# Two transformer blocks on one Trainium2 core: norm vectors moved into modulation columns, residual and gate moved into the experts' accumulators

## The chip, the cores and the metric

One core of one Trainium2 chip. The metric is the device time of one execution in microseconds (us), over which all weights are streamed once from HBM. Three runs of the kernel before gave a median of 1635.99 us (1635.38 to 1636.00). The engines are called TensorE (PE in the profile), VectorE (DVE), ScalarE (ACT), GpSimd (POOL) and SyncE (SP, which issues the loads); PEld are TensorE's weight loads.

## The reference

256 tokens of width 1024, all in float32. Block one is a parallel mixer, a cross attention and a mixture of experts, each added to x, then an RMS norm:

```
h = rms(x)*g_mix;  q,k,v,su,sv,ga,gb = split(h @ w_in)        # 3840 columns
q,k = rope(rms(q)*g_q), rope(rms(k)*g_k)
merged = sigmoid(ga)*(gqa(q,k,v) @ w_att_out) + sigmoid(gb)*(sgu(gelu(su),gelu(sv)) @ w_sgu_out)
x += merged @ w_out
x += cross(rms(x)*g_cross @ w_cq, rms(mem)*g_mem @ w_ckv) @ w_co
x += moe(rms(x)*g_moe)          # 16 experts, 2 per token, width 512
x = rms(x)*g_final
```

Block two has four sublayers s = 0..3: stick-breaking attention (16 heads), MoE, retention (8 heads, group norm, silu gate), MoE. The shift, scale and gate of each come from `silu(c) @ ada_w[s] + ada_b[s]`, 3 x 1024 numbers per sublayer:

```
x = layer_norm(alpha*x + gate_s * f_s(x*(1+scale_s) + shift_s)) * ln_g[s] + ln_b[s]     # alpha = 4**0.25
stick breaking: softplus(z) = max(z,0) + ln(1 + exp(-|z|)), its suffix sums are exponents of the weights
```

## The kernel before

**Data.** `X` (128 partitions x 2 token tiles x 1024) holds the residual stream, `XN` an RMS-normalised copy in block one. Weights arrive as 2 MB panels. A dense fp32 product is built from fp32r parts: ScalarE rounds a panel by quarters into `WHI` (`split_next`, L1117), GpSimd subtracts to `WLO` (`split_low`, L2030), and TensorE adds three products per piece. Activations are turned by `transposes` (L388, 128x128 through the identity) and split into `HTH` (ScalarE) and `HTL` (VectorE) by `turn_split` (L1132, L1486). In block two the turn also applies scale and shift, which stand as columns in `ADA` (channel on the partition).

**Loads.** SyncE issues everything in the order of `stream` (L233 ff.). Non-expert panels go round three slots of `ring_lo`: a load waits until the split of the panel three before it has read its slot. Experts use six slots. 24 panels belong to the modulation (`ada_w`, six per sublayer: two each for shift, scale and gate); `ADA_AFTER` says behind which panel each stands. TensorE takes one by `ada_panel` (L505): 8 fp32 products with silu(c) as the weights, then ScalarE copies the sums to `AROW` (`ada_copy`), TensorE turns them to columns, VectorE adds the bias (`ada_sum`, L1542). `keep_warm(n)` (L522) issues n idle products of 512 columns. SyncE also issues small vectors behind named panels (`small`); VectorE waits for all 13 of these ahead of the norm of q and k. `LNG` holds one pair of row vectors, broadcast over partitions, for the next norm's gain and bias (`gains`, L1031).

**MoE.** `moe(L)` runs on each engine: transposes of `XN` (L = 0) or `X`, router product, VectorE's choice of two experts per token, slots by a rank product, `XSPLIT` (high rows by ScalarE, low rows by GpSimd, `rows_low`, L2045), then 16 experts in 8 pairs with an extra block for overfull experts. Per expert: gather, gate and up, silu, turn, down into bank `B_Y`, `yh_out` (ScalarE) and `yl_out` (VectorE) scale by the token's weight and split, and a scatter product adds into four PSUM accumulators of 512 columns, which zero products open. After MoE 0 `residual` (L1657) adds them to X; after MoE 1 and 2 `deepnorm` (L1872) multiplies by the gate rows in `GB` (made by a diagonal and `gate_rows`, L659), adds alpha*X, takes moments, normalises, and applies gain and bias.

**Stick-breaking.** For 16 heads TensorE gives z; ScalarE takes |z|, Exp by groups of four, then four Ln of 1536 columns (three table loads with the Exp that follows); then a loop over heads: `weights` (VectorE), a suffix-sum product, Exp, value product; `values_out` copies head h-5.

**Retention.** Per head: scores, decay (VectorE), values, `stats`, `gated` (subtract mean, times silu(g)) and an in-place scaling by rstd, all on VectorE; when all 8 are done TensorE turns 16 chunks and `ret_out` runs.

The code that sets the extent of the zero products before, and the wait of q's norm:

```
for i in list(range(4)) * (2 if L else 4):
    ins = mm(acc[i], YH[0][:, 0:P], YH[0], True, False)
...
dve.wait_ge(S("small_in"), 16 * 13)
```

## Time and profile before

| what | us |
|---|---|
| median of 3 runs | 1635.99 |
| profiled execution | 1636.46 |
| its span | 1634.70 |
| TensorE busy | 1481.1 (91%) |
| VectorE busy | 532.0 (33%) |
| ScalarE busy | 463.4 (28%) |
| GpSimd busy | 423.6 (26%) |
| mean HBM traffic over the span | 273 GB/s |

The profiled execution's own time holds 1.76 us more than its span. Engines' busy times overlap, so their shares don't add up; a stage is read from a window that holds it alone. Matmul records overlap as well, and a row of the timeline can stand for several instructions (x4) of one line that follow one another.

### The profile page before, as it was taken

Reading aid. Unit: us, or ns where it says so; the run is one execution under the profiler, and the core shown is the slowest. Engines: PE = TensorE matmul, PEld = TensorE weight load, DVE = VectorE, ACT = ScalarE, POOL = GpSimd, SP = SyncE. Lnnn points to the kernel's source line nnn. Section 1 sums busy time; section 2 is a strip of 40 time slices with the busy share of each in tenths; the row PEclk is TensorE's granted clock in tenths of the full one; section 3 lists DMA queues with packets and bytes.
Section 4 is the critical chain, followed back from the end, with each engine's and each line's share of the span. In section 5 each row is a group of like instructions: output and inputs, shape, how many; then the busy total and the mean of one; then the engine's idle time right before and its main releaser. Section 6 shows DMA issues by size and latency. Waiting matters only on the chain.

```text
span 1634.7 us, 21298 instructions
## 1 busy us (share of the span) xinstructions
PE 1481.1 (91%) x7787; PEld 916.9 (56%) x7788; DVE 532.0 (33%) x1077; ACT 463.4 (28%) x792; POOL 423.6 (26%) x190
## 2 busy tenths in 40 slices
PE   7889988999999989879879999989994999999974
PEld 5777666744444479656434444369883864444431
DVE  5395424411111220236312222337008072222114
ACT  3544334211112133632211112145441321111110
POOL 5783443200000067032000000059953710000000
PEclk9999989899999989999989999989998979999997
DMA  7644365689999955518449999965541276999940
GB/s 260 226 170 154 130 238 199 254 362 426 428 429 429 374 204 199 213 37 335 169 172 423 430 428 428 365 247 194 202 158 52 103 326 260 423 429 428 429 197 26
DMA packets 89976, 447.77 MB, mean 274 GB/s; under 512 B 8212, under 2 KB 10152, under 8 KB 71336
## 3 DMA queue, kind: packets, MB, share of 16 engines
q1 hardware_dynamic: 88320, 446.17, 68.7%
q8 instruction: 55, 0.90, 0.2%
q10 hardware_dynamic: 1576, 0.49, 0.1%
q14 instruction: 25, 0.20, 0.0%
HBM read 445.60 MB, written 1.05 MB: 273 GB/s over the span
## 4 chain that ended last, share of the span: by engine, by line
PE 62%; issue 20%; DVE 11%; ACT 3%; POOL 3%; DMA 1%; DVEq 0%; POOLq 0%; ACTq 0%
PE ps L386 58%; POOL WLO L2042 2%; DVE ST L1448 1%; PE ps L718 1%; PE ps L758 1%; ACT WHI L1130 1%; PE ps L739 1%; DVE X L1889 1%; DVE X L1890 1%; DVE Z L1992 1%; PE ps L396 1%; DVE X L1883 1%; DVE SM L1880 1%; DVE Z L1580 1%; DVE Z L1581 1%
## 5 line engine op out<-in xcount | busy, mean ns | idle before, releaser
L2042 POOL TENSOR_TENSOR WLO<-ring_lo,WHI 128x1024 fp32r<-128x1024 f32 (+1 forms) x160 | 389.9, 2458 | 252.6 <-ACT WHI L1130 252.6
L386 PE MATMUL ps<-ring_hi,Z 128*64 128x512 f32 x1248 | 283.7, 604 | 5.4 <-DVE Z L1810 3.0
L386 PE MATMUL ps<-ring_lo,Z 128*64 128x512 f32 x1152 | 260.0, 601 | 5.3 <-issue 5.3
L2028 POOL TENSOR_TENSOR RS<-MS,NEGH 128x2 f32<-128x2 f32 (+1 forms) x19 | 16.1, 848 | 916.8 <-DVE MS L1458 635.9
L1130 ACT ACTIVATE WHI<-ring_lo 128x1024 fp32r<-128x1024 f32 (+1 forms) x160 | 164.6, 1048 | 234.4 <-PE ps L386 220.1
L386 PE MATMUL ps<-WHI,HTH 128*128 128x512 f32 (+1 forms) x448 | 178.4, 398 | 17.8 <-POOL WLO L2042 14.8
L386 PEld LDWEIGHTS ps<-ring_hi,Z 128*64 128x64 f32 x1248 | 88.7, 139 | 176.4 <-issue 169.8
L386 PE MATMUL ps<-WLO,HTH 128*128 128x512 f32 (+1 forms) x448 | 176.5, 394 | 0.0
L386 PE MATMUL ps<-WHI,HTL 128*128 128x512 f32 (+1 forms) x448 | 175.9, 393 | 0.0
L386 PEld LDWEIGHTS ps<-ring_lo,Z 128*64 128x64 f32 x1152 | 82.2, 138 | 156.0 <-issue 155.7
L1813 DVE TENSOR_TENSOR Z<-ps,Z 64x512 f32<-64x512 f32 x50 | 34.7, 694 | 327.1 <-ACT Z L1281 327.1
L1281 ACT ACTIVATE Z<-ps 64x512 f32<-64x512 f32 x50 | 29.5, 590 | 340.9 <-PE ps L386 340.9
L386 PEld LDWEIGHTS ps<-WHI,HTH 128*128 128x128 f32 x448 | 86.5, 193 | 38.7 <-issue 19.1
L386 PEld LDWEIGHTS ps<-WHI,HTL 128*128 128x128 f32 x448 | 86.5, 193 | 17.9
L386 PEld LDWEIGHTS ps<-WLO,HTH 128*128 128x128 f32 x448 | 86.7, 194 | 17.1
L386 PE MATMUL ps<-HTH,WHI 128*128 128x256 f32 x320 | 93.0, 291 | 0.6 <-DVE ADA L1550 0.6
L1816 DVE SCALAR_TENSOR_TENSOR YLS<-ps,Z,YHS 128x512 fp32r<-128x512 f32 x50 | 37.6, 751 | 169.0 <-ACT YHS L1287 169.0
L386 PE MATMUL ps<-HTH,WLO 128*128 128x256 f32 x320 | 91.3, 285 | 0.0
L386 PE MATMUL ps<-HTL,WHI 128*128 128x256 f32 x320 | 91.2, 285 | 0.0
L1287 ACT ACTIVATE YHS<-ps,Z 128x512 fp32r<-128x512 f32 x50 | 34.4, 687 | 184.2 <-PE ps L386 184.2
L1149 ACT ACTIVATE Z<-ps 128x512 f32<-128x512 f32 (+1 forms) x88 | 45.5, 553 | 75.6 <-PE ps L386 65.2
L386 PEld LDWEIGHTS ps<-HTH,WHI 128*128 128x128 f32 x320 | 62.5, 195 | 1.9 <-issue 1.3
(258 smaller groups left out, 1821.9 us busy)
## 6 DMA issues: line engine op xcount, KB each, us to landing
ring_lo<-in_ada_w SPq DMA_DIRECT2D x24, 2048.0 KB, 8.1
ring_lo<-in_moe_w_gate SPq DMA_DIRECT2D x16, 2048.0 KB, 10.6
ring_lo<-in_moe_w_up SPq DMA_DIRECT2D x16, 2048.0 KB, 15.0
ring_lo<-in_moe_w_down SPq DMA_DIRECT2D x16, 2048.0 KB, 14.1
ring_hi<-in_moe_w_gate SPq DMA_DIRECT2D x16, 2048.0 KB, 11.9
ring_hi<-in_moe_w_up SPq DMA_DIRECT2D x16, 2048.0 KB, 16.3
ring_hi<-in_moe_w_down SPq DMA_DIRECT2D x16, 2048.0 KB, 13.7
ring_lo<-in_ret_w_in SPq DMA_DIRECT2D x12, 2048.0 KB, 8.1
```

Of the source, the lines that this page charges most:

```text
L386: return nc.tensor.matmul(o, l, r, start=start, stop=stop, skip_group_check=True)
L396: ins = nc.tensor.transpose(o[:, at:at + P], src(t, c), ident)
L718: ins = nc.tensor.transpose(ps[:, bank, j * P:(j + 1) * P], ROWS[h][:, j * P:(j + 1) * P], ident)
L739: ins = nc.tensor.transpose(ps[:, bank, t * P:(t + 1) * P], sel[:, t, :], ident)
L758: ins = nc.tensor.transpose(ps[:, B_GU, c * CAP:(c + 1) * CAP], by4[CAP:P, c, :], CST[CAP:P, C_ID + CAP:C_ID + P])
L1130: nc.scalar.activation(WHI[:, q, 0:size], slot(r)[:, q * size:(q + 1) * size], Copy).then_inc(S("hi_split"), 1)
L1149: drain(nc.scalar.activation(dst, o[:, src], func, **k), key)
L1281: nc.scalar.activation(SG[a][CAP:P, :], ps[0:CAP, B_GU, :], ACT.Silu).then_inc(done, 1)
L1287: nc.scalar.activation(YH[a], ps[:, B_Y, :], Copy, scale=WSLOT[a]).then_inc(done, 1)
L1813: V.tensor_tensor(HH[a][CAP:P, :], ps[CAP:P, B_GU, :], SG[a][CAP:P, :], ALU.mult).then_inc(done, 1)
L1816: V.scalar_tensor_tensor(out=YL[a], in0=ps[:, B_Y, :], scalar=WSLOT[a], in1=YH[a].bitcast(F32), op0=ALU.mult, op1=ALU.subtract).then_inc(d ...
L2042: nc.gpsimd.tensor_tensor(WLO[:, q, 0:size], slot(r)[:, q * size:(q + 1) * size], WHI[:, q, 0:size].bitcast(F32), ALU.subtract).then_inc(S ...
```

## The change

- `ADA_AFTER` and the calls that use up the panels: new places for 20 of the 24 modulation panels, the first now ahead of `in q`; other counts for `keep_warm`.
- Norm gains and biases of the sublayer before go into the `ADA` scale and shift columns (`ada_sum`, with `LNM`, `VT` from three new loads at the start, `FOLD`). `XN` is then the normalised, ungained value throughout and is what gets turned and gathered. Four more small loads stand behind `in ga1`, and q's norm waits for 17.
- `carry(k)` on VectorE computes alpha*(XN*g+b) into X; in the MoEs TensorE opens the accumulators with `ident x X` in four fp32 products.
- In MoE 1 and 2 the gate is multiplied per expert (`yf_out`), with rows from `gate_halves`; `moe_norm` reads the accumulators in PSUM. `layer_norm` stands behind sb_out and ret_out. The output leaves in two halves.
- Stick-breaking: VectorE takes -|z| of heads 4 to 7; Exp and Ln of heads 8 to 15 go into the last loop; `values_out` copies head h-7.
- Retention: ScalarE scales by rstd; each head is turned and split inside the loop.

```diff
-    ADA_AFTER = {("in", "gb1"): (0,), ("sgu_out", 0): (1, 2, 3), ("w_out", 1): (4, 5), ("cq", 0): (6,), ("co", 0): (7, 8), ("moe", 0): (9, 10, 11),
-                 ("sb", 5): (12, 13, 14, 15), ("sb_out", 1): (16, 17), ("moe", 1): (18, 19, 20, 21), ("ret_out", 3): (22, 23)}
+    ADA_AFTER = {("ckv", 1): (0,), ("in", "gb1"): (1, 2), ("w_out", 0): (3, 4), ("w_out", 1): (5, 6), ("cq", 0): (7,), ("co", 0): (8, 9, 10),
+                 ("moe", 0): (11, 12), ("sb", 5): (13, 14), ("sb_out", 1): (15, 16, 17, 18), ("moe", 1): (19, 20), ("ret_out", 3): (21, 22, 23)}
...
         project(("ckv", 1))
+        ada_panels_now(0)
         pe.wait_ge(S("xn_ready"), 2)
         transposes("x", lambda t, c: XN[:, t, c * P:(c + 1) * P], KC)
-        keep_warm(3)
+        ada_flush()
+        keep_warm(2)
...
-        ada_panels_now(1, 2, 3)
+        ada_panels_now(3, 4)
+        keep_warm(3)
...
+        def gate_halves(s):
+            pe.wait_ge(S("diag"), s + 1)
+            o = claim(pe, ("gate", s, 0), "B")
+            for h in range(2):
+                ins = mm(o[64 * h:64 * h + 64, :], cst(C_ONES, 64), GB[:, h * 512:(h + 1) * 512], True, True)
+            fill(ins, ("gate", s, 0))
...
             acc = [claim(pe, ("y", L, i), "A") for i in range(4)]
-            pe.wait_ge(S("acc_zero"), L + 1)
             if L:
-                gate_rows(2 * L - 1)
-            for i in list(range(4)) * (2 if L else 4):
-                ins = mm(acc[i], YH[0][:, 0:P], YH[0], True, False)
+                gate_halves(2 * L - 1)
+                pe.wait_ge(S("x_ready"), 2 * L)
+            for i in range(4):
+                ins = mm(acc[i], ident, X[:, i // 2, 512 * (i % 2):512 * (i % 2) + 512], True, False)
+                if i == 2:
+                    ins.then_inc(m(L, "x_gu"), 1)
             ins.then_inc(m(L, "xdone"), 1)
-            mm(acc[3], YH[0][:, 0:P], YH[0], True, False).then_inc(m(L, "x_gu"), 1)
...
-                keep_warm((2, 6)[L])
+                keep_warm((2, 2)[L])
...
-            ada_panels_now(16, 17)
-            keep_warm(12)
+            ada_panels_now(15, 16, 17, 18)
+            keep_warm(4)
...
+            def ret_turn(h):
+                pe.wait_ge(S("ret_scaled"), h + 1)
+                o = claim(pe, ("ro", h), "B")
+                for k in range(2):
+                    for t in range(NT):
+                        ins = nc.tensor.transpose(o[:, k * SEQ + t * P:k * SEQ + (t + 1) * P], RG[:, t, 256 * h + k * P:256 * h + (k + 1) * P], ident)
+                fill(ins, ("ro", h))
             ret_scores(0)
+            ret_scores(1)
             for h in range(8):
-                if h < 7:
-                    ret_scores(h + 1)
                 ret_values(h)
+                if h < 6:
+                    ret_scores(h + 2)
+                if h >= 2:
+                    ret_turn(h - 2)
+            ret_turn(6)
+            ret_turn(7)
...
+        for r, v in ((V_FIN, A["g_final"]), (V_LG, A["ln_g_2"][0, 1]), (V_LB, A["ln_b_2"][0, 1])):
+            sp.dma_start(VROW[r:r + 8, 0, :], v.rearrange("(k p) -> k p", p=P)).then_inc(S("norm_vec_in"), 16)
...
+            ("in", "ga1"): [(LNM[:, i, r, :], A[v][i, 0].rearrange("(p c) -> p c", c=KC)) for i in range(2) for r, v in enumerate(("ln_g_2", "ln_b_2"))]}
...
-        sp.dma_start(out.rearrange("o (t p) d -> p (o t) d", p=P), X[:, :, :]).then_inc(S("stored"), 16)
-        sp.wait_ge(S("stored"), 16)
+        for t in range(NT):
+            sp.wait_ge(S("out_ready"), t + 1)
+            sp.dma_start(out[0, t * P:(t + 1) * P, :], X[:, t, :]).then_inc(S("stored"), 16)
...
             def yh_out(a, done):
+                if L:
+                    nc.scalar.activation(YH[a], SG[a], Copy).then_inc(done, 1)
+                    return
                 nc.scalar.activation(YH[a], ps[:, B_Y, :], Copy, scale=WSLOT[a]).then_inc(done, 1)
...
+            def exps(q):
+                g = SE[:, 4 * q:4 * q + 4, :]
+                for h in range(4 * q, 4 * q + 4):
                     read(act, ("z1", h))
-                    g = SE[:, h - 3:h + 1, :]
-                    nc.scalar.activation(g, g, ACT.Exp, scale=-1.0).then_inc(S("exp_abs"), 1)
-            for q in range(4):
+                nc.scalar.activation(g, g, ACT.Exp, scale=1.0 if q == 1 else -1.0).then_inc(S("exp_abs"), 1)
+            def logs(q):
                 act.wait_ge(S("exp_abs"), q + 1)
                 g = SE[:, 4 * q:4 * q + 4, :]
                 nc.scalar.activation(g, g, ACT.Ln, bias=1.0).then_inc(S("log1p"), 1)
+            for h in [*range(4), *range(8, 16)]:
+                move(("z1", h), SE[:, h, :], slice(0, 384), ACT.Abs)
+                if h == 3:
+                    exps(0)
+            exps(1)
+            logs(0)
+            logs(1)
...
+                if h == 1:
+                    exps(2)
+                elif h == 3:
+                    exps(3)
+                    logs(2)
+                    logs(3)
...
+            for h in range(8):
+                act.wait_ge(S("rstd"), RET_NORMS + h + 1)
+                read(act, ("rv", h))
+                for t in range(NT):
+                    v = RG[:, t, 256 * h:256 * h + 256]
+                    ins = nc.scalar.activation(v, v, Copy, scale=RS[:, h % 2, t:t + 1])
+                ins.then_inc(S("ret_scaled"), 1)
+                if h >= 1:
+                    turn_split("ro", 2 * h, 0, h - 1)
+            turn_split("ro", 16, 0, 7)
...
+                for k in range(n - 3, n):
+                    read(dve, ("adac", k))
+                link(V.tensor_scalar(v, v, 1.0, None, ALU.add))
+                s = n // 6
+                gain = VT[:, 0, V_FIN:V_FIN + 8] if s == 0 else VT[:, 0, V_LG:V_LG + 8] if s == 2 else LNM[:, s // 2, 0, :]
+                bias = VT[:, 0, V_LB:V_LB + 8] if s == 2 else LNM[:, s // 2, 1, :]
+                if s:
+                    shift = ADA[:, 24 * s:24 * s + 8]
+                    link(V.tensor_tensor(FOLD[:, :], bias, v, ALU.mult))
+                    V.tensor_tensor(shift, shift, FOLD[:, :], ALU.add)
+                V.tensor_tensor(v, v, gain, ALU.mult).then_inc(S("ada_scale"), 1)
...
+        ada_sum(0)
+        dve.wait_ge(S("small_in"), 16 * 17)
...
+                carry(2 * L)
                 diag(2 * L - 1)
...
+            def yf_out(a, done):
+                V.scalar_tensor_tensor(out=SG[a], in0=ps[:, B_Y, :], scalar=WSLOT[a], in1=GB[:, 0:512],
+                                       op0=ALU.mult, op1=ALU.mult).then_inc(done, 1)
             def yl_out(a, done):
+                if L:
+                    V.tensor_tensor(YL[a], SG[a], YH[a].bitcast(F32), ALU.subtract).then_inc(done, 1)
+                    return
                 V.scalar_tensor_tensor(out=YL[a], in0=ps[:, B_Y, :], scalar=WSLOT[a], in1=YH[a].bitcast(F32),
                                        op0=ALU.mult, op1=ALU.subtract).then_inc(done, 1)
...
+        def carry(k):
+            dve.wait_ge(S("gains_in"), 16 if k == 1 else 16 + 32 * (k - 1))
+            for t in range(NT):
+                v = X[:, t, :]
+                ins = V.scalar_tensor_tensor(out=v, in0=XN[:, t, :], scalar=ALPHA, in1=LNG[:, 0, :], op0=ALU.mult, op1=ALU.mult)
+                if k > 1:
+                    link(ins)
+                    ins = V.scalar_tensor_tensor(out=v, in0=LNG[:, 1, :], scalar=ALPHA, in1=v, op0=ALU.mult, op1=ALU.add)
+            ins.then_inc(S("x_ready"), 1)
+            dve.wait_ge(S("x_ready"), k)
...
+        def moe_norm(L, sums=()):
+            def piece(t, h):
+                return result(dve, ("y", L, 2 * t + h))
+            n = moments(None, D, EPS_LN if L else EPS_RMS, L == 0, 0, piece)
+            for a in sums:
+                ada_sum(a)
+            rstd(n)
+            for t in range(NT):
+                for h in range(2):
+                    v = XN[:, t, 512 * h:512 * h + 512]
+                    if L:
+                        ins = V.tensor_scalar(v, piece(t, h), MV[:, 0, t, 0:1], RS[:, 0, t:t + 1], ALU.subtract, ALU.mult)
+                    else:
+                        ins = V.tensor_scalar(v, piece(t, h), RS[:, 0, t:t + 1], None, ALU.mult)
+                    drain(ins, ("y", L, 2 * t + h))
+                if L == 2:
+                    dve.wait_ge(S("gains_in"), 16 + 32 * 4)
+                    for h in range(2):
+                        read(dve, ("y", L, 2 * t + h))
+                    link(V.tensor_tensor(X[:, t, :], XN[:, t, :], LNG[:, 0, :], ALU.mult))
+                    V.tensor_tensor(X[:, t, :], X[:, t, :], LNG[:, 1, :], ALU.add).then_inc(S("out_ready"), 1)
...
+            for h in range(4, 8):
+                o = result(dve, ("z1", h))[:, 0:384]
+                link(V.tensor_scalar(SE[:, h, :], o, -1.0, None, ALU.mult))
+                ins = V.scalar_tensor_tensor(out=SE[:, h, :], in0=o, scalar=1.0, in1=SE[:, h, :], op0=ALU.mult, op1=ALU.min)
+                drain(ins, ("z1", h))
...
-                if h % 2 and h >= 5:
-                    values_out(h - 5)
-                    values_out(h - 4)
-            for h in range(12, 16):
+                if h % 2 and h >= 7:
+                    values_out(h - 7)
+                    values_out(h - 6)
...
             for h in range(8):
-                if h < 7:
-                    decayed(h + 1)
-                k_[h] = stats(h)
-                if h >= 1:
-                    gated(h - 1, k_[h - 1])
-            gated(7, k_[7])
-            turn_split("ro", 16)
-            deepnorm(lambda t, h: ("ret_out", "o", t, h), 2, 3)
+                stats(h)
+                gated(h)
+                if h < 6:
+                    decayed(h + 2)
+                if h >= 2:
+                    turn_split("ro", 2 * h - 2, 0, h - 2)
+            turn_split("ro", 16, 0, 6)
+            layer_norm(2, (21,))
```

## Rows read from the trace of the kernel before

**Rows 1.** The page, part 4: the ended-last chain, share of the span by engine.

```profile
PE 62%; issue 20%; DVE 11%; ACT 3%; POOL 3%; DMA 1%; DVEq 0%; POOLq 0%; ACTq 0%
```

**Rows 2.** Windows: start:end, length, busy PE, PEld, DVE, ACT, POOL (count), clock, DMA share, GB/s.

```profile
329.50:560.00 230.50, 227.15 (x1168) 101.64 (x1168) 39.92 (x89) 42.11 (x94) 0.00 (x0) 1.00 0.98 413
560.00:586.30 26.30, 17.57 (x107) 10.59 (x105) 19.11 (x32) 9.33 (x15) 10.41 (x5) 0.81 0.96 348
...
656.00:723.30 67.30, 52.11 (x419) 39.14 (x417) 25.25 (x57) 39.45 (x65) 2.53 (x2) 0.95 0.33 126
...
747.00:787.50 40.50, 34.48 (x161) 21.59 (x153) 29.74 (x93) 11.23 (x17) 6.86 (x3) 0.87 0.70 285
...
1048.60:1084.30 35.70, 29.10 (x168) 16.23 (x169) 22.60 (x38) 10.04 (x16) 9.98 (x5) 0.77 0.96 356
...
1612.70:1634.70 22.00, 1.20 (x8) 0.67 (x8) 14.98 (x21) 0.00 (x0) 0.70 (x1) 0.61 0.12 48
```

**Rows 3.** Timeline around in q: start, duration, engine, line, operation [idle <- released by].

```profile
40.35 2.96 ACT L1130 ACTIVATE WHI<-ring_lo 128x1024 fp32r<-128x1024 f32 x3 [5.18 <-DMA ring_lo<-in_w_in]
...
50.82 0.47 PE L386 MATMUL ps<-WHI,HTH 128*128 128x512 f32 x1
```

**Rows 4.** Timeline of VectorE, SyncE, TensorE; then landings of the small WR loads.

```profile
70.06 1.50 DVE L1561 TENSOR_TENSOR Z<-Z 128x1280 f32<-128x1280 f32 x1 [13.01 <-ACT Z L1184]
...
76.22 0.38 SPq L1015 DMA_DIRECT2D ring_lo<-in_w_in  x1
...
119.74 0.77 PE L386 MATMUL ps<-WHI,HTH 128*128 128x512 f32 x1 [3.44 <-POOL WLO L2042]
...
DMA to landing us min/median/max: 6.9/7.5/11.5
```

**Rows 5.** Chain of waits, 199 to 240, its load of w_out.

```profile
199.79 7.92 DMA ring_lo<-in_w_out
```

**Rows 6.** Chain of waits, then VectorE's timeline, 559 to 586.

```profile
562.06 8.05 DMA ring_lo<-in_sb_w_in
...
559.71 2.48 DVE L1661 TENSOR_TENSOR X<-ps,X 128x512 f32<-128x512 f32 x4 [0.83 <-PE ps L386]
...
576.14 2.78 DVE L1498 TENSOR_TENSOR HTL<-hT,HTH 128x512 fp32r<-128x512 f32 x1
```

**Rows 7.** Timeline of ScalarE and VectorE, stick-breaking attention.

```profile
671.88 1.28 ACT L1366 ACT_TABLE_LOAD   x1
673.17 5.60 ACT L1366 ACTIVATE Z<-Z 128x1536 f32<-128x1536 f32 x4
...
690.85 0.88 DVE L1928 TENSOR_TENSOR HTL<-ps,HTH 64x256 fp32r<-64x256 f32 x2 [6.81 <-ACT HTH L1370]
...
696.07 0.88 DVE L1928 TENSOR_TENSOR HTL<-ps,HTH 64x256 fp32r<-64x256 f32 x2 [2.37 <-ACT HTH L1370]
```

**Rows 8.** Timeline of TensorE, GpSimd and VectorE, entry of MoE 1; last, behind it.

```profile
761.26 2.06 PE L396 MATMUL ps<-CST,X 128*128 128x128 f32 x16 [0.39 <-DVE X L1890]
...
766.04 3.36 POOL L2052 TENSOR_TENSOR XSPLIT<-X,XSPLIT 128x1024 fp32r<-128x1024 f32 x1 [11.57 <-ACT XSPLIT L1253]
...
770.36 1.90 DVE L1720 TENSOR_TENSOR Z<-Z 128x32 f32<-128x32 f32 x1
...
1060.10 1.23 DVE L1889 TENSOR_TENSOR X<-X,LNG 128x1024 f32<-128x1024 f32 x1
```

**Rows 9.** Timeline of ScalarE, a silu of MoE 0.

```profile
550.94 0.59 ACT L1281 ACTIVATE Z<-ps 64x512 f32<-64x512 f32 x1 [6.18 <-PE ps L386]
```

**Rows 10.** Timeline of TensorE, warming products behind MoE 1.

```profile
1066.19 7.91 PE L386 MATMUL ps<-CST 128*128 128x512 f32 x12 [4.08 <-DVE ADA L1548]
```

**Rows 11.** Timeline of VectorE and TensorE, end of the retention.

```profile
1247.64 4.37 DVE L1992 TENSOR_SCALAR Z<-Z,RS 128x256 f32<-128x256 f32 x2
...
1266.34 0.77 PE L386 MATMUL ps<-WHI,HTH 128*128 128x512 f32 x1 [3.06 <-DVE ROL L1504]
```

**Rows 12.** DMA issues: output, count, KB each, us from issue to landing.

```profile
out_x<-X SPq DMA_DIRECT2D x1, 1024.0 KB, 4.0
```

227 lines of the change are left out of this document (111 added, 116 removed).

## The prediction, made before the changed kernel was run

> **What bounds the kernel now.** I read the chain of waits first. Of the path that ended last, TensorE holds 62%, `issue` 20%, VectorE 11% and all DMA together 1% [rows 1]: the kernel is a row of TensorE stages with small-work gaps between them, and no queue limits it overall. The table by stage shows which stages can move [rows 2]. In the expert stage (329.5 to 560) TensorE is busy 227.15 of 230.50 us at full granted clock, so such a stage only shifts with its start. The seams are loose: 17.57 of 26.30 busy behind the first MoE, 52.11 of 67.30 in the stick-breaking attention, 34.48 of 40.50 at the entry of the second MoE, 29.10 of 35.70 behind it, 1.20 of 22.00 in the tail, with granted clocks of 0.61 to 0.95 where TensorE had been idle. Nearly all edits lie in seams, so I work out for each when the next dense TensorE stage can start; the table is cut where such a stage now starts or ends. In the experts 2 MB panels flow at 413 GB/s, 2.097 MB / 0.413 = 5.1 us each [rows 2]; that spacing prices every reordering of loads.
>
> **Terms** (us; minus is faster; in brackets the bounds).
>
> *Front, ada 0 before `in q`.* ScalarE begins q's split at 40.35, after 5.18 idle for that very load, and TensorE starts q at 50.82 [rows 3]. With a panel ahead q lands about 5.1 later; behind it ScalarE now also has two moves for ckv and one for the ada bank in order ahead of the turns of x, some 1.9 more. **+7** (4 to 8.5; 4 if part of the 5.1 is absorbed while x is turned).
>
> *Norm vectors by DMA.* Four small loads are queued on SP behind `in ga1`, and VectorE's q/k norm now waits for all 17 small loads. That norm starts at 70.06, and SP issues ga1 only at 76.22 [rows 4]. Small 64 KB loads took 6.9 to 11.5 us to land [rows 4]. Counted without the front's shift, which moves both sides: issued at about 75 (POOL's split ends 1.2 sooner with VectorE silent), they land at about 82.5. Three operations follow, the first 1.50, together about 3.7, then POOL's rstd, which now starts behind a split at 76.14 and would start at 86: 10 late, with VectorE's twelve rope operations behind it and POOL's splits of sv and on to gb0, whose product starts at 119.74 after 3.44 idle for POOL [rows 4]. Splits that no longer meet the norm give half a microsecond back. **+9.5** (0, if they land in time, a case below, to 12).
>
> *w_out.* Its load is 7.92 of the chain from 199.79 on, behind three ada panels [rows 5]. None of them stays in front: it lands one panel's 5.1 earlier, as far as a freed slot allows; w_out's second half then waits for the split that frees its slot, which gives 1.3 back. **-3.8** (-5.5 to -1.5). MoE 0's entry: no zero fill beyond 4 products, one panel fewer in front of the transposes: **-1** (-2 to 0).
>
> *MoE 0 to stick-breaking.* The residual, 4 x 0.62 = 2.48 [rows 6], is gone because X already sits in the accumulators, and one of three ada panels ahead of `sb 0` is gone: its load is on the chain for 8.05 from 562.06, to 570.1 [rows 6], and now takes the place of the third panel, which was issued long before. After that the norm (statistics, rstd, four scalings) bounds, at 2.48 less, and the wait for the split of a late panel goes too, some 2.5. The turn's 512-column TENSOR_TENSOR of 2.78 beside POOL [rows 6] stays. **-5** (-6 to -3).
>
> *Stick-breaking softplus.* Before, a pair of heads takes 696.07 - 690.85 = 5.22 us in the last loop [rows 7], each value waiting for ScalarE. Ln for heads 8 to 15 now comes inside the loop, so the first weights come earlier by two Exp/Ln groups (5.60 / 4 = 1.40 each [rows 7], less what |z| on VectorE adds), values lag one more pair, and the loop runs at what ScalarE needs, about 4.1 to 4.3. Eight pairs save about 8; two more table loads at 1.28 [rows 7] and 2 x 1.4 of work moved into the loop come back. **-6.5** (-9.5 to -4). The table load row ends at 673.16 and the next ACTIVATE starts at 673.17 [rows 7]: nothing of a switch lies outside it. The Trainium skill ("ScalarE: Activation LUTs", What ACT_TABLE_LOAD costs) adds a drain of about 1380 ns to a load of 1283 ns; by that the step would be worth 2.7 less. The trace has the load and not the drain, so I keep the row.
>
> *sb_out to MoE 1.* VectorE loses two passes per tile, 4 x 1.23 = 4.9 [rows 8]: xn is ready near 756.3 instead of 761. But PE has four ada panels in front instead of two (the last can only load when a slot is freed, and lands about 756.6) and four warming products at low clock: transposes begin about 762 to 765, against 761.26 [rows 8]. Then `carry(2)`, four operations of 1024 elements at 1.23, stands ahead of the routing chain on VectorE, beside POOL's two splits, the first 3.36 [rows 8]. Beside POOL an operation of 32 columns took 1.90 at 770.36, while 1024 columns without POOL take 1.23 [rows 8]; so I let the four alternate with POOL's operations: the last ends about 7.5 after the first can start, and routing is read about 7 later than now (770.36 is its second step); 1.7 comes back at that stalled operation, and 2.5 from a clock that is then higher. Four identity products in fp32 replace nine fp32r ones: about equal. **+6** (-3 to +9). The Trainium skill ("SBUF — State Buffer", Who interferes with whom) says that a VectorE instruction with two SBUF inputs contends with a GpSimd one that reads SBUF, as an exclusive lock for the whole instruction, and thus speaks against this carry; the rows agree in kind, by the 1.90 for 32 columns, and for a 1024-element instruction no row shows it.
>
> *MoE 1 and 2, the extra block and the end.* y of an expert now goes PSUM x GB on VectorE, a ScalarE copy, a VectorE subtraction: one operation of about 0.70 more on the path from down to scatter. In the pairs it lies beside the next expert's gate and up: ScalarE idles 6.18 for TensorE ahead of each silu [rows 9]. It shows only where nothing follows: **+1.4** each (0 to 3). Without that cover it is the slower rival below.
>
> *MoE 1 to retention.* Two ada panels instead of four and 2 warming products for 6: these 6 and what went with them took 7.91 at low clock from 1066.19 on, behind 4.08 idle for the panels' sums [rows 10]. The seam behind MoE 0 has three panels and 2 warming products, and takes 26.3 now and 21.3 by the step above; this one takes 35.7 [rows 2]. With two panels and the load ahead it becomes like that one, plus 1.2 for subtracting means: 22.5. **-13.2** (-15 to -11). `carry(3)` comes behind the turns, where no product waits for it.
>
> *Retention's outputs.* Before, all 32 turns wait for the last in-place scalings, which begin at 1247.64 and take 4.37 for two beside POOL (the next two are alike), and the product starts at 1266.34 [rows 11]. Now ScalarE scales (two ACTIVATEs a head) and each head is turned two heads later. Left behind the last gating are a scaling, 4 turns and their split, together about 4: 1251.6, and the loop ends 0.7 later for the work put into it. 1252.3 - 1266.3 = **-14** (-15.5 to -8).
>
> *ret_out to MoE 2*: norm passes -5, carry and its neighbours +5, third panel and cold start against fewer warming products: **-2** (-5 to +2). *Tail:* 22.00 us in which TensorE does 1.20 [rows 2]. Multiplying by the gate and adding X fall away (8 operations on PSUM tiles at 0.62 [rows 6], 5.0), scaling from PSUM adds little, and the output transfer of 1 MB, 4.0 [rows 12], goes half under the second tile, with a second issue. **-4.8** (-6 to -3.5).
>
> **Sum.** 7 + 9.5 - 3.8 - 1 - 5 - 6.5 + 6 + 1.4 - 13.2 - 14 - 2 + 1.4 - 4.8 = -25.0. The profiled run took 1636.46 (span 1634.70 and 1.76 around it), 0.5 above the median of 1635.99 of the shown runs. 1636.0 - 25.0 = **1611**. Its own range, with independent errors of about half of each bracket: 1604 to 1619.
>
> **Rivals.**
> 1. *The carry hides.* The two-input operations run at 1.23 beside POOL, or end before its splits start. For: POOL's first split waits 11.57 for ScalarE, so two of four could be done. Against: the 1.90 for 32 columns. The two entries lose 4.5 each: 1611 - 9 = 1602. Chance 0.15.
> 2. *The norm vectors land in time,* because ga1 is issued once its slot is free and the front's delay moves VectorE more than SP. For: 6.9 is the low end of landings. Against: SP is in order. The term of 9.5 goes: 1601.5. Chance 0.15.
> 3. *The new loops are bound elsewhere.* ScalarE gets two scalings and a turn-split per head in retention beside ret_out's splitting, and the stick-breaking loop keeps a serial wait: retention -7 and softplus -1.5 instead of -14 and -6.5, 1623; with the late bounds of both MoE entries as well (+3, +7) it reaches 1633. Chance 0.14.
> 4. *Slower: the y step opens the expert loop.* It lies between down and scatter in every expert of two MoEs. It decides from the point where y's chain exceeds the cover of 6.18 [rows 9]; it is three operations of 0.6 to 0.75, about 2.1, and waits of its own could add to it. Then every expert pays the two operations that follow one another, 1.44: 32 x 1.44 = 46, 1657. Against: TensorE had only 3.35 us idle in 230. Chance 0.05.
> 5. Remaining 0.51 for the forecast.
>
> Faster or slower than 0.2% (3.3 us) is what a measurement of this kernel can tell from no change. Faster is all of cases 1, 2, 5 and of case 3 all but 0.03: 0.92; within: 0.03; slower: 0.05. The range 1598 to 1625 takes in cases 1 and 2 with their lower flank and most of 3, and leaves out 4, the tail of 3 and a doubly lucky case.
>
> **What would show it.** In the trace after: q's first product near 57.5; the q/k norm waiting for a DMA and starting near 89; `in gb0` at about 136; w_out near 226; sb 0 at about 593; the pair period of the stick-breaking loop near 4.2; the routing of MoE 1 read 7 us later behind its transposes than before, with carry's operations longer than 1.23 beside POOL; no idle between the experts of MoE 1; retention's first product near 1079; ret_out's product 5 us behind the last gating. The forecast falls if MoE 0 does not start about 12 us late, or if any MoE stage's TensorE share falls below 0.95.

## The result, and the profile after

The changed kernel takes 1616.38 us in the median of 4 runs (1613.27 to 1619.56), the kernel before 1635.68: ratio 0.9885, 95% interval 0.9864 to 0.9906, or 19 us faster. The forecast was 1611, with a range of 1598 to 1625. The profiled execution took 1615.90, its span 1614.0, so the two traces differ by 20.7 us.

The page's chain of the changed kernel, which answers to [rows 1]: VectorE's share has fallen from 11% to 7%, DMA's risen from 1% to 3%.

```profile
PE 61%; issue 20%; DVE 7%; POOL 4%; ACT 4%; DMA 3%; DVEq 0%; SPq 0%; POOLq 0%; ACTq 0%
```

The windows of the changed kernel (start:end, length, busy PE, PEld, DVE, ACT, POOL with counts, granted clock, DMA share, GB/s) are, in order: MoE 0, the seam behind it (a seam is the small work between two dense stages), the stick-breaking attention, from the first modulation panel behind sb_out to MoE 1, MoE 1, the seam behind it, the end of the retention, MoE 2, the tail. Those that [rows 2] has too are cut at the same events; MoE 1, the end of the retention and MoE 2 stand here alone.

```profile
338.90:569.40 230.50, 227.15 (x1168) 101.35 (x1168) 39.94 (x89) 42.12 (x94) 0.00 (x0) 1.00 0.98 413
569.40:589.70 20.30, 13.31 (x75) 7.55 (x73) 16.40 (x26) 8.63 (x14) 10.44 (x5) 0.84 0.65 232
659.80:719.50 59.70, 46.16 (x370) 36.94 (x369) 27.56 (x60) 40.15 (x62) 2.52 (x2) 0.94 0.19 71
743.00:791.60 48.60, 35.35 (x199) 20.87 (x198) 33.22 (x98) 11.92 (x18) 7.34 (x3) 0.82 0.81 324
791.60:1052.70 261.10, 247.12 (x1241) 108.17 (x1241) 64.65 (x127) 43.84 (x100) 0.00 (x0) 0.98 0.87 361
1052.70:1076.00 23.30, 16.90 (x96) 9.63 (x97) 17.00 (x25) 8.63 (x14) 10.43 (x5) 0.75 0.53 192
1210.50:1244.90 34.40, 24.20 (x118) 18.91 (x116) 26.14 (x80) 18.74 (x39) 10.57 (x11) 0.91 0.01 1
1332.80:1598.10 265.30, 251.29 (x1239) 109.96 (x1239) 64.64 (x127) 43.83 (x100) 0.00 (x0) 0.96 0.79 333
1598.10:1614.00 15.90, 1.19 (x8) 0.67 (x8) 10.81 (x15) 0.00 (x0) 0.70 (x1) 0.57 0.16 66
```

MoE 0 is the same to the hundredth, 227.15 busy in 230.5. The two seams behind MoEs are 6 and 12 us shorter, the entry of MoE 1 is longer, with TensorE busy for 35.35 of 48.60. Placed one after the other, the starts of the dense stages give the ledger, in us (first TensorE product of each, from the two timelines; a MoE ends here where its last scatter product starts; the stretches add up to the spans):

| stretch, from - to | before | after | difference | forecast |
|---|---|---|---|---|
| start - `in q` | 50.8 | 58.1 | +7.3 | +7 |
| - att_out | 123.7 | 132.0 | +8.3 | +9.5 |
| - first expert of MoE 0 | 155.0 | 148.8 | -6.1 | -4.8 |
| MoE 0 | 230.3 | 230.2 | 0.0 | 0 |
| - sb 0 | 26.5 | 20.6 | -6.0 | -5 |
| - sb_out | 137.0 | 129.8 | -7.2 | -6.5 |
| - first expert of MoE 1 | 64.2 | 72.2 | +8.0 | +6 |
| MoE 1 | 261.9 | 261.8 | -0.1 | +1.4 |
| - ret 0 | 34.9 | 22.5 | -12.4 | -13.2 |
| - ret_out | 182.0 | 168.8 | -13.2 | -14 |
| - first expert of MoE 2 | 88.7 | 87.9 | -0.8 | -2 |
| MoE 2 | 258.6 | 266.2 | +7.6 | +1.4 |
| tail | 21.1 | 15.1 | -6.0 | -4.8 |

Twelve of the thirteen lines lie within 2 us of the forecast; the one that doesn't is MoE 2, 6.2 off. Time is lost at the front (+15.6), at the entry of MoE 1 and in MoE 2, and gained in every other place. Each column is one execution, and a stretch whose code didn't change can differ between executions by several us: in the kernels of the experiments that leave the stick-breaking code and its two panels as in the changed kernel, this stretch takes 129.7 to 134.5. A line that fits to within 2 us is not a proof of its term; the experiments and the rows have to give that.

At the front, timelines of ScalarE, SyncE, VectorE and TensorE answer to [rows 3] and [rows 4]:

```profile
45.67 3.90 ACT L1160 ACTIVATE WHI<-ring_lo 128x1024 fp32r<-128x1024 f32 x4 [10.50 <-DMA ring_lo<-in_w_in]
...
82.55 0.58 SPq L1079 DMA_DIRECT2D LNM<-in_ln_g  x1
...
90.93 1.49 DVE L1635 TENSOR_TENSOR Z<-Z 128x1280 f32<-128x1280 f32 x1 [26.53 <-DMA LNM<-in_ln_b]
...
100.21 0.77 PE L389 MATMUL ps<-WHI,HTH 128*128 128x512 f32 x1 [13.88 <-POOL WLO L2156]
```

q's split starts at 45.67 and not 40.35: 5.3 for one panel ahead. VectorE then stands still for 26.53 us until the norm vectors' loads, issued from 82.55 on, have landed; GpSimd gets its rstd late, and TensorE waits 13.88 for its split in place of 2.5.

At the entry of MoE 1, TensorE, VectorE and GpSimd answer to [rows 8]:

```profile
753.09 3.08 PE L389 MATMUL ps<-ring_lo,SILC 128*32 128x512 f32 x16 [2.57 <-DMA ring_lo<-in_ada_w]
756.10 4.20 PE L389 MATMUL ps<-CST 128*128 128x512 f32 x8
760.13 1.93 PE L399 MATMUL ps<-CST,Z 128*128 128x128 f32 x16
764.96 4.84 PE L389 MATMUL ps<-WR,hT 128*128 128x16 f32 x32
776.43 1.97 PE L389 MATMUL ps<-GB,CST 128*64 128x512 f32 x4 [6.63 <-DVE GB L1763]
...
750.83 1.54 DVE L1992 TENSOR_SCALAR Z<-X,MV,RS 128x1024 f32<-128x1024 f32 x2
...
765.15 3.59 DVE L1967 SCALAR_TENSOR_TENSOR X<-Z,LNG 128x1024 f32<-128x1024 f32 x1
768.77 3.75 DVE L1970 SCALAR_TENSOR_TENSOR X<-LNG,X 128x1024 f32<-128x1024 f32 x1
772.45 1.21 DVE L1967 SCALAR_TENSOR_TENSOR X<-Z,LNG 128x1024 f32<-128x1024 f32 x1
773.69 1.23 DVE L1970 SCALAR_TENSOR_TENSOR X<-LNG,X 128x1024 f32<-128x1024 f32 x1
...
764.79 2.86 POOL L2166 TENSOR_TENSOR XSPLIT<-Z,XSPLIT 128x1024 fp32r<-128x1024 f32 x1 [14.00 <-ACT XSPLIT L1282]
767.60 3.84 POOL L2166 TENSOR_TENSOR XSPLIT_last<-Z,XSPLIT 128x1024 fp32r<-128x1024 f32 x1
```

Two things are to be seen. The normalised value was ready at 752.4, the transposes began at 760.13 behind the fourth panel. And of carry's four operations the two beside GpSimd take 3.59 and 3.75, the two without it 1.21 and 1.23; TensorE, which has the router's product done at 769.8, is idle 6.63 until 776.43.

### The profile page after: what moved, and what is told of

Same layout as the page of the kernel before. It is cut to its first block, busy times and chain, and to the rows that moved or that the text cites. A ratio compares the mean times of both kernels' runs of the same rounds, so it can differ in the third digit from the quotient of the medians.

```text
span 1614.0 us, 21322 instructions
## 1 busy us (share of the span) xinstructions
PE 1461.7 (91%) x7736; PEld 898.5 (56%) x7737; DVE 543.1 (34%) x1096; ACT 468.3 (29%) x806; POOL 424.1 (26%) x190
## 4 chain that ended last, share of the span: by engine, by line
PE 61%; issue 20%; DVE 7%; POOL 4%; ACT 4%; DMA 3%; DVEq 0%; SPq 0%; POOLq 0%; ACTq 0%
PE ps L389 58%; POOL WLO L2156 3%; ACT WHI L1160 1%; DMA ring_lo<-in_w_in 1%; PE ps L731 1%; PE ps L771 1%; PE ps L752 1%; DMA ring_lo<-in_w_cq 1%; DVE ST L1508 1%; DVE Z L1655 1%; DVE Z L1654 1%; DVE Z L1653 1%; DMA ring_lo<-in_ada_w 0%; DMA ring_lo<-in_w_out 0%; PE ps L399 0%
## 5 line engine op out<-in xcount | busy, mean ns | idle before, releaser
L2142 POOL TENSOR_TENSOR RS<-MS,NEGH 128x2 f32<-128x2 f32 (+1 forms) x19 | 16.1, 847 | 922.5 <-DVE MS L1518 637.7
L389 PEld LDWEIGHTS ps<-ring_hi,Z 128*64 128x64 f32 x1248 | 87.8, 138 | 175.5 <-issue 168.8
L389 PE MATMUL ps<-Z 64*128 64x256 f32 (+7 forms) x312 | 51.2, 386 | 18.0 <-DVE Z L1861 8.5
L1317 ACT ACTIVATE YHS<-Z 128x512 fp32r<-128x512 f32 x34 | 21.4, 629 | 152.5 <-DVE Z L1891 152.5
```

The lines of the kernel that those rows point to most:

```text
L389: return nc.tensor.matmul(o, l, r, start=start, stop=stop, skip_group_check=True)
L1317: nc.scalar.activation(YH[a], SG[a], Copy).then_inc(done, 1)
```

## The experiments

The changed kernel's 1616.4 is the reference for those that edit it; all ratios are to the kernel before, run beside each. "Stretch" is a line of the table above. The changed kernel's own ratio has the interval 0.9864 to 0.9906, and a single edit worth 5 to 7 us has one that touches or overlaps it, so for these the starts of the stages in the traces decide, and not the median alone.

**Own wait for the norm vectors.**

```diff
-                    sp.dma_start(dst, row).then_inc(S("small_in"), 16)
+                    sp.dma_start(dst, row).then_inc(S("lnm_in" if key == ("in", "ga1") else "small_in"), 16)
...
+                if n == 9:
+                    dve.wait_ge(S("lnm_in"), 16 * 4)
...
-        dve.wait_ge(S("small_in"), 16 * 17)
+        dve.wait_ge(S("small_in"), 16 * 13)
```

> The changed kernel with one wait moved: the four loads of the norm vectors signal a semaphore of their own, which is waited for at the first modulation sum that reads them (panel 9), and the q/k norm waits for 13 small loads as before. Order and number of loads are unchanged. If the wait for these loads is what shifted everything between q and attention by 7.95 us, the time falls by 7 to 8.5 us, q's norm starts about 13 us earlier and the 13.88 us idle ahead of sv shrinks to about 4. Rival: the stage is bound by GpSimd's splits anyway and the wait only covers for them; then the time falls by less than 2.

1609.42 us, ratio 0.9847 (0.9811 to 0.9884), 7.0 less. VectorE's and TensorE's timelines of this kernel:

```profile
77.91 1.67 DVE L1637 TENSOR_TENSOR Z<-Z 128x1280 f32<-128x1280 f32 x1 [12.65 <-ACT Z L1215]
...
90.16 0.76 PE L389 MATMUL ps<-WHI,HTH 128*128 128x512 f32 x1 [2.51 <-POOL WLO L2158]
```

The norm starts 13.0 earlier, sv 10.1 earlier, attention's output product 8.7 earlier (181.35 against 190.04), and MoE 0 starts 8.5 earlier. The term was the wait's own: the stretch from q to att_out had grown by 8.3.

**Panel 0 behind w_in again.**

```diff
-    ADA_AFTER = {("ckv", 1): (0,), ("in", "gb1"): (1, 2), ("w_out", 0): (3, 4), ("w_out", 1): (5, 6), ...
+    ADA_AFTER = {("in", "gb1"): (0, 1), ("w_out", 0): (2, 3), ("w_out", 1): (4, 5), ("cq", 0): (6,), ...
-                 ("moe", 0): (11, 12), ("sb", 5): (13, 14), ...
+                 ("moe", 0): (10, 11), ("sb", 5): (12, 13, 14), ...
...
```

The calls that use up the panels move with them.

> The changed kernel with modulation panel 0 back behind the last panel of w_in, and every panel up to 12 one place later than in the change (so the stick-breaking stage takes three instead of two). If panel 0 in front of q is worth the 7.3 us by which q's first product came later, q starts at 50.8 again and the time falls by 5.5 to 7.5 us (the third panel at stick-breaking costs up to 1.9). Rival: the displaced panels collide later (attention, w_out, cq), and less than 3 us is left of it.

1610.38 us, ratio 0.9859 (0.9833 to 0.9885), 6.0 less. q starts at 50.03, 8.1 earlier; the 8.1 are still there at att_out, 7.1 at MoE 0; the stick-breaking stretch with a third panel takes 134.4 instead of 129.8, but it takes 134.4 and 134.5 in two kernels with two panels as well, so this trace doesn't show what the third panel costs.

**Carry ahead of the turn.**

```diff
+            if L > 0:
+                dve.wait_ge(S("xn_ready"), 4 + L)
+                carry(2 * L)
             turn_out(("moe", L), KC, lambda c: hT[:, c, :])
...
-                carry(2 * L)
                 diag(2 * L - 1)
```

> The changed kernel with VectorE's carry (alpha*(XN*g+b) into X) of MoE 1 and 2 moved ahead of the turned activations, into the time in which VectorE waits for TensorE, instead of ahead of the routing chain beside GpSimd's row splits. If the carry beside GpSimd is what holds the routing (its operations took 3.6 to 3.8 instead of 1.2, TensorE idle 6.6 ahead of the gate product), the four operations take 1.2 each, the idle falls to under 1.5 at both entries, and the time falls by 9 to 12 us. Rival: the entry is held by the modulation panels and the turning, and the routing chain meets GpSimd in the carry's place; then 3 us or less.

1611.09 us, ratio 0.9847 (0.982 to 0.9874): 5.3 less, half of what I expected. VectorE's and TensorE's timelines at MoE 1, then TensorE's at MoE 2:

```profile
759.64 1.22 DVE L1969 SCALAR_TENSOR_TENSOR X<-Z,LNG 128x1024 f32<-128x1024 f32 x1
760.90 1.23 DVE L1972 SCALAR_TENSOR_TENSOR X<-LNG,X 128x1024 f32<-128x1024 f32 x1
...
772.49 3.57 DVE L1763 TENSOR_TENSOR GB<-CST,ADA 128x1024 f32<-128x1024 f32 x1
...
772.30 7.01 PE L389 MATMUL ps<-WR,hT 128*128 128x16 f32 x32
779.24 1.98 PE L389 MATMUL ps<-GB,CST 128*64 128x512 f32 x4
...
1310.62 1.32 PE L389 MATMUL ps<-CST,AROW 128*128 128x1 f32 x8 [1.54 <-DVE hT L1537]
```

The mechanism is as expected: carry at 1.2, the 6.63 idle gone, router to first expert 23.0 and 22.9 instead of 26.7 and 27.8. But the lock (two engines shutting each other out for whole instructions) has moved to the diagonal (3.57 instead of 1.23). At MoE 1 that costs nothing, since VectorE then waits 3.29 for the router's product; it is late itself, for its 32 small products take 7.01 where they took 4.84, at the lower clock, and 2.2 are lost there. At MoE 2 carry now holds the turned activations up: TensorE waits 1.54 for them, and the router's product comes 61.8 behind ret_out's first instead of 60.1. From sb_out and ret_out to the first expert the two entries are 3.0 and 3.2 shorter, 6.2 together. The profiled execution (1616.96, the longest of the four) doesn't show that in its total: the untouched stick-breaking stretch takes 134.4 there and MoE 1 takes 264.2.

**The three together** (the three diffs above).

> All three edits together. If they act on different seams the gains add: 7.5 + 6.5 + 10.5 = 24.5, about 1592. If the front edits overlap (panel 0 and the norm vectors' wait hide one another) it is some 5 less, 1597.

1600.27 us, ratio 0.9787 (0.9768 to 0.9806): 16.1 less. The medians of the three singles add to 18.3, which fits with different seams within the noise; I had put them at 24.5. The windows from the router's first product to the first expert of MoE 0 show where a part stays, first this kernel, then the changed one:

```profile
307.49:329.46 21.97, 19.08 (x68) 14.11 (x67) 13.75 (x61) 4.14 (x8) 4.71 (x2) 0.63 1.00 425
```

```profile
321.20:338.88 17.68, 14.80 (x69) 10.52 (x68) 11.83 (x59) 4.70 (x8) 5.32 (x2) 0.81 1.01 431
```

The same products run at a granted clock of 0.63 instead of 0.81 and take 4.3 longer. They are the larger part of what the whole stretch from att_out to MoE 0 has lost (154.7 instead of 148.8).

**The retention part alone**, on the kernel before (the hunks of the diff at `ret_turn`, `ret_scaled` and the loop over heads).

> The kernel before with the retention part of the change alone (ScalarE scales by rstd, each head is turned and split inside the loop, scores two heads ahead). The prediction gave it 14 us; in the changed kernel's trace the stretch from retention's first product to ret_out's first went from 182.0 to 168.8. If that is this edit's own, the stretch is 168.8 here too and the time falls by 13, to about 1622.5. Rival: part of the 13 comes from the other edits around it; then less than 8, and the stretch over 173.

1624.52 us, ratio 0.9933 (0.9912 to 0.9955), 12.0 less than 1636.55; the stretch is 168.4. TensorE's timeline of this kernel at the loop's end answers to [rows 11]:

```profile
1247.03 1.12 PE L975 MATMUL ps<-CST,Z 128*128 128x128 f32 x4 [2.39 <-ACT Z L1432]
1250.60 0.77 PE L387 MATMUL ps<-WHI,HTH 128*128 128x512 f32 x1 [2.46 <-POOL WLO L2059]
```

Four turns and 2.46 us stand between the last head and ret_out. The gain is the edit's own.

**Stick-breaking part alone**, on the kernel before (`exps`, `logs`, |z| on VectorE, values one pair later).

> The kernel before with the stick-breaking part of the change alone (|z| of heads 4 to 7 on VectorE, Exp and Ln of heads 8 to 15 inside the last loop, values copied one pair later); the four modulation panels stay between the logits. The prediction gave the part 6.5 us; in the changed kernel's trace the stretch from sb's first product to sb_out's went from 137.0 to 129.8, in other runs to 132 to 134 with the panels placed otherwise. Mine: pairs at 4.0 instead of 5.2 us, the stretch at 130 to 132, the time down by 5 to 7, to about 1630. Rival: the part owes its gain to having two panels less there; then less than 3 us.

1629.30 us, ratio 0.9966 (0.9951 to 0.9981), 6.2 less than 1635.45. The values' subtractions on VectorE, with [rows 7] for before:

```profile
694.90 0.88 DVE L1942 TENSOR_TENSOR HTL<-ps,HTH 64x256 fp32r<-64x256 f32 x2 [2.09 <-ACT HTH L1378]
...
698.90 0.88 DVE L1942 TENSOR_TENSOR HTL<-ps,HTH 64x256 fp32r<-64x256 f32 x2 [1.12 <-ACT HTH L1378]
```

Pairs follow each other by 4.00 us, not 5.22. The stretch is 133.1, 3.9 less than before, a little longer than I had said; the rest of the 6.2 lies in places that the edit doesn't touch. From the first pair's weights to the last pair's, VectorE needs 30.5 us in this kernel and in the changed one, 37.6 before: the loop gives 7.1. Behind it 1.9 come back, because the values lag one more pair, and 1.3 are lost ahead of it.

**A longer gate step**, against the slower rival.

```diff
             def yf_out(a, done):
+                for k in range(2 * L):
+                    V.scalar_tensor_tensor(out=X[:, k // 2, 512 * (k % 2):512 * (k % 2) + 512], in0=ps[:, B_Y, :], scalar=WSLOT[a], in1=GB[:, 0:512],
+                                           op0=ALU.mult, op1=ALU.mult)
```

> The changed kernel with useless copies of VectorE's gate multiplication ahead of it, written to X, which is free then: two more per expert in MoE 1 (+1.4 us in the chain from down to scatter, 4.3 in all), four more in MoE 2 (+2.9, 5.8 in all). If the next expert's gate and up cover the chain as long as it stays under 6.2 us, the pairs stay at 28.73 us in both, and only the extra block and the last expert pay: about 2 x 1.4 and 2 x 2.9, 8 to 9 us in all, 1625. Rival (the slower case of the prediction): the chain is open already; then each expert pays what is added, 16 x 1.4 + 16 x 2.9 = 69, 1685.

1634.03 us, ratio 1.0013 (0.9992 to 1.0034): 17.7 more. The windows of one pair in MoE 1 and two in MoE 2, then TensorE's timeline behind the extra block of MoE 2:

```profile
898.07:926.80 28.73, 28.73 (x149) 12.91 (x149) 10.66 (x20) 5.30 (x12) 0.00 (x0) 1.00 1.00 427
1382.38:1439.87 57.49, 57.49 (x298) 25.87 (x297) 26.58 (x48) 10.60 (x24) 0.00 (x0) 1.00 1.00 426
...
1580.05 0.79 PE L389 MATMUL ps<-YHS,SELTS 64*128 64x512 f32 x2 [4.97 <-DVE YLS L1899]
```

A pair takes 28.73 us whether two, four or no operations are added: the next expert's products cover them, and the rival is out. The idle time shows in three places per MoE (ahead of the extra block, at its scatter, at the last one), not two: 4.34, 2.33 and 2.24 in the changed kernel's MoE 2, 6.99, 4.97 and 4.88 here, 7.9 in all; 3.6 in MoE 1. The other 6 of the 17.7 lie almost all in MoE 1 (5.4), where the 38 us around the extra block ran at a granted clock of 0.78 instead of 0.91 and a block of 32 products took 9.4 instead of 8.8. That the longer gaps are what lowered the clock is argued, not isolated: MoE 2 had the longer ones and lost no more than its idle time.

**Carry behind the turn, GpSimd's splits held.**

```diff
             turn_out(("moe", L), KC, lambda c: hT[:, c, :])
+            if L > 0:
+                carry(2 * L)
...
-                carry(2 * L)
                 diag(2 * L - 1)
...
+            if L:
+                pool.wait_ge(S("x_ready"), 2 * L)
             for t in range(NT):
                 pool.wait_ge(S("rows_high"), NT * L + t + 1)
```

> The changed kernel with carry directly behind VectorE's turned activations and GpSimd's two row splits of MoE 1 and 2 waiting until it is done. If the two engines lock each other out, the four operations take 1.2 each as they did when moved earlier, and the stretch from the router product to the first expert falls from 26.7 and 27.8 to about 23 at both entries: 8 us in all, 1609. Rival: the delayed row splits hold the gather in the carry's place; then the stretch stays above 26 and nothing is gained.

1617.56 us, ratio 0.9883 (0.9861 to 0.9904): nothing gained by time, though the operations take 1.2. Router to first expert is 23.5 at MoE 1 (26.7 in the changed kernel), but 27.0 at MoE 2 (27.8), where two modulation sums stand between carry and diagonal and the splits, now released, meet these. VectorE and GpSimd at MoE 2:

```profile
1313.05 1.23 DVE L1971 SCALAR_TENSOR_TENSOR X<-LNG,X 128x1024 f32<-128x1024 f32 x1
1314.31 0.23 DVE L1610 TENSOR_TENSOR ADA<-ps,VT 128x4 f32<-128x4 f32 x2
1314.58 2.65 DVE L1615 TENSOR_SCALAR ADA<-ADA 128x8 f32<-128x8 f32 x1
1317.26 3.82 DVE L1763 TENSOR_TENSOR GB<-CST,ADA 128x1024 f32<-128x1024 f32 x1
...
1314.36 2.84 POOL L2169 TENSOR_TENSOR XSPLIT<-Z,XSPLIT 128x1024 fp32r<-128x1024 f32 x1 [11.09 <-DVE X L1971]
```

An operation of eight columns takes 2.65 there. The 4 us that the two entries gained in this trace are outweighed by stretches that the edit doesn't touch: the stick-breaking one takes 134.5 at a granted clock of 0.93, 129.8 at 0.97 in the changed kernel.

**Panel 15 moved forward**, `("sb", 5): (13, 14, 15), ("sb_out", 1): (16, 17, 18)`.

> The changed kernel with modulation panel 15 taken from behind sb_out and put with 13 and 14 behind the stick-breaking logits, so that three panels instead of four stand ahead of MoE 1. XN was ready at 752.3 there and TensorE's transposes began at 760.1, behind the fourth panel (landed 753.1) and four warming products. If that panel holds the entry, the stretch from sb_out's first product to the router's falls from 45.5 to about 39, and the time by 5 to 7 us. Rival: without the panel the entry is held by XN or a lower clock; less than 2.5 us.

1617.98 us, ratio 0.9906 (0.9871 to 0.9941), and two runs near 1611.6 with two near 1625: by time this is inconclusive. In its trace (1611.7) sb_out to router takes 38.7 instead of 45.5, as said: the fourth panel held the entry. The stick-breaking stretch takes 132.6, within what it takes with two panels.

**All of it**, three versions of the combination; the diff has the two places in which the second differs from the first. The second puts the four panels between the stick-breaking logits and holds the splits until the diagonal; the third takes each MoE entry in the form that was shortest.

```diff
             for j in range(8):
                 logits("z1", j, True)
+                if j % 2:
+                    ada_panel(12 + j // 2, "A")
...
-                pool.wait_ge(S("x_ready"), 2 * L)
+                pool.wait_ge(S("diag"), 2 * L)
```

> All of it on the changed kernel: own wait for the norm vectors, panel 0 late, four panels behind the stick-breaking logits and three behind sb_out, carry behind the turn with GpSimd's row splits held until it is done. The three edits run before took 1616.4 to 1600.3. Three panels instead of four at the second MoE's entry should give 6.5 more, the fourth panel at stick-breaking take 0 to 2 back: about 1595. Rival: seams already moved share their gain with a low granted clock behind the shorter idle, and it stays within 2 of 1600.

> The version of all edits again, with two places mended that its trace showed: the four panels stand between the stick-breaking logits (behind them the fourth had to wait for a slot, and the stretch took 145.4), and GpSimd's row splits wait for VectorE's diagonal as well (in MoE 2 the lock had only moved to it, 3.8 instead of 1.2). Stick-breaking at 131 to 133 is 13 less, MoE 2's entry at 23 to 24 instead of 27 is 3.5 less: 1604.1 - 16.5 = 1588. Rival: a lower clock behind the shorter gaps takes part of it back; 1595.

> The second best version with each MoE entry in the form that was shortest: in MoE 1 carry behind the turn and GpSimd's row splits held until carry (not the diagonal) is done, router product to first expert 23.5 instead of 26.1; in MoE 2 carry ahead of the turn and nothing held, ret_out's first product to the first expert 84.5 instead of 85.9. That is 4 us on 1597.3, so 1593.5. Rival: the two entries' differences lay in the granted clock of those runs; then it stays at 1597 within 2.

1604.05 (ratio 0.9805, 0.9779 to 0.9831), 1597.34 (0.9762, 0.9744 to 0.978) and 1594.10 us (0.9747, 0.9731 to 0.9764). In the first, TensorE's timeline shows the fourth panel waiting for a slot of the ring, with three panels in a row ahead of it, and the stretch took 145.4:

```profile
667.01 3.64 PE L389 MATMUL ps<-ring_lo,SILC 128*32 128x512 f32 x16 [3.90 <-DMA ring_lo<-in_ada_w]
```

Between the logits it took 133.8. Holding the splits for the diagonal too made router to first expert 26.1 instead of 23.5 at MoE 1, and 25.9 instead of 27.1 at MoE 2. At MoE 1 the gather didn't wait for the splits, which had ended 8 us before it; its products and the turns behind it ran at the lower clock (the first three 1.62 instead of 0.93), and 2.1 of the 2.5 lie there. The third is 22 us faster than the changed kernel, 41 than the kernel before.

## Why the prediction was right, and where it was off

*Front and norm vectors, +16.5 forecast, +15.6 measured.* Both steps hold singly: -8.1 at q without the panel in front, -8.7 at att_out without the shared wait. The two medians (-7.0 and -6.0) agree, and don't prove it alone. Rival 2 (the vectors land in time) is out: VectorE waited 26.53 for them. The norm started at 90.93 (forecast 89). The prediction is said to fall if MoE 0 doesn't start about 12 late. It started 9.4 late, so that sign came, narrowly: the front cost 1 less than forecast and the next step gained 1.3 more.

*w_out and MoE 0's entry, -4.8 forecast, -6.1 measured.* No panel stands ahead of w_out's first half any more, and its first product comes 36.8 behind att_out's instead of 42.0: the 5.1 of one panel. The second half's load is what stands on the chain now (229.15, when its slot comes free), then cq's (9.29 from 247.72), and 1.0 has come back when cq starts. These two steps are as forecast. The other 2.0 lie between router and first expert, where there are fewer zero products and the granted clock was 0.81 and not 0.74. That this place alone varies by 4.3 with the clock (the three-edit version), and that with unchanged code the whole stretch took 151.8 to 155.0 (stick-breaking part alone, kernel before), makes the agreement of the total partly luck. (Of the 24 panels 13 have changed place, not 20.)

*MoE 0 to stick-breaking, -5 forecast, -6.0 measured, softplus -6.5 forecast, -7.2 measured.* The first has no experiment of its own. In the second, the pair period of 4.00 is a little under the 4.1 to 4.3 said, and holds in the part run alone, but only for the last pairs, behind the Exp and Ln that moved into the loop. That run had a stretch of 133.1 and -3.9 at the same granted clock of 0.97, so some 3 of the 7.2 go with the two panels less in this place: the part itself was worth less than forecast (the lag of one more pair costs 1.9 at its end, for which the prediction has no price), and the panels made up for it. The 129.8 is also at the low end of what this code takes: five kernels with it and two panels took 129.7 to 134.5, mean 132.1, at clocks of 0.97 to 0.93. By the mean the gain is 4.9, still in the range of the term; that the trace gave 7.2 was luck.

*sb_out to MoE 1, +6 forecast, +8.0 measured.* Both halves of the step are in the trace: the fourth panel (transposes 7.8 after XN was ready; forecast 762 to 765 in the old frame, 763.9 in it) and carry beside GpSimd. VectorE read the router's result at 776.1, 6.3 after it was there. The version with one panel fewer ahead of the entry confirms the first half (6.8 from sb_out to router), those with carry moved the second. Rival 1 (carry hides) is out by 3.59 and 3.75. The Trainium skill ("SBUF — State Buffer", Who interferes with whom) says that a VectorE instruction with two SBUF inputs and a GpSimd one that reads SBUF exclude one another for a whole instruction; the traces agree for 1024 columns: 1.2 without GpSimd in three kernels, 3.6 to 3.9 beside it. That little (0.8) was won in MoE 2 by shielding carry alone agrees too.

*The y step, +1.4 forecast for each MoE, -0.1 and +7.6 measured.* This is the term that was mis-sized. TensorE's timeline of MoE 2, the kernel before and then the changed one, ahead of the extra block, at its scatter and at the last one:

```profile
1561.08 1.94 PE L386 MATMUL ps<-X,Z 128*64 128x512 f32 x8 [3.61 <-DVE Z L1786]
1582.99 0.51 PE L386 MATMUL ps<-YHS,SELTS 64*128 64x512 f32 x2 [1.67 <-DVE YLS L1816]
1612.75 0.50 PE L386 MATMUL ps<-YHS,SELTS 64*128 64x512 f32 x2 [1.57 <-DVE YLS L1816]
...
1541.43 2.96 PE L389 MATMUL ps<-Z 128*64 128x512 f32 x8 [4.34 <-DVE Z L1861]
1566.23 0.79 PE L389 MATMUL ps<-YHS,SELTS 64*128 64x512 f32 x2 [2.33 <-DVE YLS L1896]
1598.14 0.50 PE L389 MATMUL ps<-YHS,SELTS 64*128 64x512 f32 x2 [2.24 <-DVE YLS L1896]
```

By idle times the step costs 2.1 in MoE 2 and 2.4 in MoE 1 (3.13 to 4.20, 1.67 to 2.33, 1.57 to 2.24): the prediction had one operation of 0.70 at two places, and there are three. The -0.1 and the 7.6 are not its work alone. In the six MoE 1 and 2 stretches with unchanged MoE code (the kernel before, retention alone, softplus alone) it took 258.3 to 263.4, mean 261.0, with 258.6 in the trace that the forecast started from; in the twenty with the changed MoE code and no added copies 260.2 to 267.2, mean 263.4. So 2.4 is the step's own, in agreement with the idle times, and 2.4 is what the start value of MoE 2 was below the mean; the rest is within the spread (the granted clock ahead of the extra block of MoE 2 was 1.00 before and 0.84 after; what it is due to stays open). MoE 2 lies 6.2 above its forecast: 1.0 by the step's size, 2.4 by the start value, 2.8 by the spread. MoE 1 took what it did before because the same two worked the other way there. The second sign of a fall came here: TensorE's share in MoE 1 and 2 is 0.946 and 0.947, under the 0.95 that was set, from 0.956 and 0.954 before, by these gaps and not by an open expert loop.

*MoE 1 to retention -13.2 forecast, -12.4 measured; retention's end -14 forecast, -13.2 measured, -12.0 when run alone.* The size is right in both. For the retention the run of the part alone shows the mechanism; for the seam behind MoE 1 (fewer panels, fewer warming products) no run isolates it. Rival 3 (another engine binds) decides nothing here: behind the last gating (1239.36) 5.5 us pass, 1.5 more than said, for ScalarE's scaling and GpSimd's last split.

*Entry of MoE 2 and tail.* The entry gave -0.8, forecast -2, with 6.56 idle ahead of the gate product, as at MoE 1. The tail gave 6.0, not 4.8: its statistics read PSUM and the first half of the output leaves while the second tile is normalised. No run isolates it.

*Rival 4* (the expert loop opens) is refuted with room to spare: four more operations per expert changed no pair.

The total, 5 us above the forecast and well inside the range, thus holds an error of 6 in one line and several that cancel.

## What to carry to other kernels

A wait on a count that several loads share makes the earliest consumer wait for the latest load: give a late load its own semaphore. Here that took 8.7 us off the stretch and cost nothing that the trace shows. Work that is moved off an engine's busy stretch gains only if it lands where its neighbour engine is silent; here the same four operations cost 5 or 10 us by their place alone, and shielding them passed the stall to the next in line. Price a chain's extra step by counting the places where nothing covers it, and take a stage's start value from several executions. The same holds for a hit: one trace whose stretch fits the forecast may owe that to its clock.
